# Fill matmuls of the identity with itself on TensorE, ahead of waits, in a one-core encoder kernel

## The chip, the cores and the metric

The kernel runs on one core of one Trainium2 chip. A core has a matrix engine (TensorE, PE in the rows; its weight loads are PEld), VectorE (DVE), ScalarE (ACT), GpSimd (POOL) and SyncE (SP), which run side by side and wait for one another through semaphores, and 16 DMA engines. The metric is the device time of one launch in microseconds (us). For a profiled execution the profile gives the span from the first to the last instruction, and the run its time, which has what lies around the span too.

TensorE's clock is granted at one of two levels, 1.2 or 2.4 GHz. The rows name it as PEclk, 0.50 or 1.00 of full speed for a stretch; a mean lies between.

## The reference

One encoder layer in fp32, applied to two sequences of their own, a prompt of 256 tokens and a sample of 512, model width 1024:

```python
h = rmsnorm(x, norm_mix_g)
q, k, v, z_sg, gate_logits = split(h @ w_in)
attn_branch = block_attention(rope(rmsnorm(q)), rope(rmsnorm(k)), v) @ w_attn_o
sg_branch = spatial_gating(gelu(z_sg), sg_norm_g, sg_w, sg_b) @ w_sg_o
x = x + (sigmoid(g_a) * attn_branch + sigmoid(g_s) * sg_branch) @ w_out
x = x + cross_attention(rmsnorm(x, norm_xa_g), rmsnorm(mem, norm_mem_g), wq_xa, wkv_xa, wo_xa)
x = x + peer_ffn(rmsnorm(x, norm_ffn_g), w_peer_q, peer_k1, peer_k2, expert_down, expert_up)
```

Self-attention has 16 query heads and 4 key heads of 64; cross-attention 4 heads of 256 over 256 memory rows. `peer_ffn` picks, for each token and each of 8 heads, 16 of 16384 experts and sums their rows with gates. A last rmsnorm gives the two outputs.

## The kernel before

Tokens are tiles of 128. The prompt (2 tiles) goes first and the sample (4 tiles) second through the same stages, called the first and the second pass here (`q.first` is true in the first; `NT` is 2 or 4): `mixer_inputs` (L561 to 753), `self_attention`, `mixer_outputs`, `cross_inputs`, `cross_attention`, and then `routing` in the first pass or `routing_and_gates` in the second. `experts` and `final_norm` follow once for all tokens. Each stage writes one instruction stream for each engine; a stream runs in the order in which it is written, and an instruction behind a wait waits too.

Three helpers carry most of TensorE's work.

- `project_tokens` and `project_features` multiply a turned activation by streamed weights. A weight chunk of 512 columns comes in two halves; ScalarE writes a half's high part (`split_hi`, L182, w_hi) and VectorE its low part (`split_lo`, L188, w_lo), and each product is three fp32r matmuls (`three`, L203 to 205). Ahead of each half TensorE waits for the low part (`lo_done`, L214), and from the second chunk on it also waits, tile by tile, until the tile's bank of the chunk before is read out (`o.freed`, L217).
- `Turn` transposes a token-major tile into feature-major blocks in 8 steps of up to 4 tiles, with six banks in turn (L276): ScalarE copies each step out as T_hi (L284), VectorE writes T_lo (L292), and from step 6 on TensorE waits for the T_lo of the step six before. `turn.wait` waits for the last.
- In `self_attention` a step of the loop issues the scores of pair `step`, then the turn (transposes, L947) of pair `step - 2`, then the values (L959) of pair `step - 3`. In the generic `attention` that cross-attention uses the order is the same, with L807, L816 and L827. They differ in what the scores wait for:

```python
                if p >= 2:
                    pe.wait_ge(exped, 2 * p - 2)      # self_attention, scores(p)
                if u >= 3:
                    pe.wait_ge(exped, u - 2)          # attention, scores(u)
```

In the second pass VectorE also does background work: products of gathered expert rows (L135), a number of them written at fixed places of its stream (`bg.dve`), whose rows GpSimd fetches by indirect DMA into a ring of six.

In `mixer_outputs` the attention output projection (evicted at L1161 with a gate), eight spatial-gating matmuls (L1107, evicted at L1179), the turn of their result, the second projection, the turn of the gated sum and the output projection follow one another.

Of the kernel before, what the change touches and what calls it, by code (L numbers as in the profile page):

```python
# [16 lines left out]
P = 128  # L17
# [5 lines left out]
NT = (SAMPLE + PROMPT) // P  # L23
# [181 lines left out]
    return pe.matmul(out, lhs[1], rhs[0], start=False, stop=stop, skip_group_check=True)  # L205


def project_tokens(pe, st, h0, nchunks, T, tiles, lin, o, between=None):

    n = len(tiles)  # L210
    for c in range(nchunks):
        for half in range(2):
            h = h0 + 2 * c + half
            pe.wait_ge(st.lo_done, h + 1)  # L214
            for i, t in enumerate(tiles):
                if half == 0 and c > 0:
                    pe.wait_ge(o.freed, n * (c - 1) + i + 1)  # L217
                for k in range(HK):
                    cols = slice(t * P, (t + 1) * P)
                    kk = half * HK + k  # L220
                    last = three(pe, lin[:, i, :], (T[0][:, kk, cols], T[1][:, kk, cols]),
                                 (st.hi[:, h % 2, k, :], st.lo[:, h % 2, k, :]),
                                 start=(kk == 0), stop=(kk == KB - 1))
                if half == 1:
                    last.then_inc(o.ready, 1)
                elif i == n - 1:
                    last.then_inc(st.used, 1)
                if half == 0 and between is not None:
                    between(c, i)
# [28 lines left out]
class Turn:  # L258
# [6 lines left out]
        (self.turned, self.base), (self.hi, _), (self.lo, _) = (  # L265
            m.carried(x, len(self.steps)) for x in ("turned", "turn_hi", "turn_lo"))

    def pe(self, pe, before=None):

        for n, (k, t0, nt) in enumerate(self.steps):  # L270
            if before is not None:
                before(n, t0 + nt)
            if n >= 6:
                pe.wait_ge(self.lo, self.base + n - 5)
            for t in range(nt):
                last = pe.transpose(self.lin[:, n % 6, t * P:(t + 1) * P],  # L276
                                    self.src[:, t0 + t, k * P:(k + 1) * P], self.ident[:])
            last.then_inc(self.turned, 1)
# [235 lines left out]
def mixer_inputs(nc, block, st, q, bg, x_in, T, Y, qT, kT, v_sb, lin, tr, A, U, GA, GS, stage, ident, gains, choice=None, norm=None, routed=None):  # L514
    NT, H = q.nt, q.h0
    Y = Y[:, q.t0:q.t0 + NT, :]
    Pool.next_stage()

    with ExitStack() as ctx:
# [48 lines left out]
        @block.tensor  # L568
        def _(pe):
            if q.first:  # L570
                pe.wait_ge(turn_in, 32)
            turn.pe(pe, lambda n, end: pe.wait_ge(norm.scaled, norm.base + end))
            turn.wait(pe)
            if not q.first:
                routed(pe)

            def qk_turn(n):
                pe.wait_ge(roped, n + 1)
                if n >= 2:
                    pe.wait_ge(copied, n - 1)  # L580
                for b in range(4):
                    last = pe.transpose(tr[:, n % 2, b * P:(b + 1) * P], rope[:, n % 2, b * P:(b + 1) * P], ident[:])
                last.then_inc(turned, 1)

            def between(c, i):
                if 1 <= c <= 3:
                    qk_turn((c - 1) * NT + i)

            project_tokens(pe, st, H, 11, T, range(NT), lin, o, between)
# [186 lines left out]
def attention(nc, block, tag, bg, T, ident, lin, tr, units, heads, outs, width_of, scores_of, crossed):  # L776
# [8 lines left out]
    with ExitStack() as ctx:  # L785
# [14 lines left out]
        @block.tensor  # L800
        def _(pe):
            def scores(u):
                if u >= 3:
                    pe.wait_ge(exped, u - 2)
                pairs = scores_of(units[u])
                for i, (a, b) in enumerate(pairs):
                    last = pe.matmul(lin[:, u % 3, 0:width_of(units[u])], a, b, start=(i == 0),  # L807
                                     stop=(i == len(pairs) - 1))
                last.then_inc(scored, 1)

            def turn(u):
                pe.wait_ge(normed, u + 1)
                if u >= 3:
                    pe.wait_ge(copied, u - 2)
                for kb in range(width_of(units[u]) // P):
                    last = pe.transpose(lin[:, 3 + u % 3, kb * P:(kb + 1) * P],  # L816
                                        probs[:, u % 3, kb * P:(kb + 1) * P], ident[:])
                last.then_inc(turned, 1)

            def values(u):  # L820
                pe.wait_ge(copied, u + 1)
                h, t = head_of[units[u][:2]], units[u][2]
                for p in (p for p in outs if p["head"] == h):
                    if t == 0 and p["opens"] and p["bank"] >= 2:
                        pe.wait_ge(out_lo, p["bank"] - 1)
                    for kb, v in enumerate(p["values"]):
                        last = pe.matmul(tr[p["rows"], p["bank"] % 2, t * P:(t + 1) * P], v, pT[:, u % 3, kb, :],  # L827
                                         start=(kb == 0), stop=(kb == len(p["values"]) - 1))
                last.then_inc(valued, 1)

            crossed(pe)
            for step in range(N + 3):
                if step < N:
                    scores(step)
                if 2 <= step < N + 2:
                    turn(step - 2)
                if 3 <= step:
                    values(step - 3)
# [69 lines left out]
def self_attention(nc, block, q, bg, T, qT, kT, v_sb, ident, lin, tr, projected):  # L908

    with ExitStack() as ctx:  # L910
# [14 lines left out]
        def _(pe):  # L925
# [40 lines left out]
            for step in range(N + 3):  # L966
                if step < N:
                    scores(step)
                if 2 <= step < N + 2:
                    turn(step - 2)  # L970
                if 3 <= step:
                    values(step - 3)
# [66 lines left out]
        return attended  # L1039


def mixer_outputs(nc, block, st, q, bg, T, Y, G, lin, A, U, GA, GS, ident, cleared, attended, spills_done):
    NT, H = q.nt, q.h0 + 2 * W_AO
    Y = Y[:, q.t0:q.t0 + NT, :]

    with ExitStack() as ctx:
# [50 lines left out]
        @block.tensor  # L1097
        def _(pe):
            attended(pe)
            project_tokens(pe, st, H, 2, T, range(NT), lin, o)  # L1100
            norm.wait(pe)
            pe.wait_ge(small_in, 48)
            pe.wait_ge(o.freed, NO)
            for g in range(G_SG):
                if g >= 6:
                    pe.wait_ge(sg_done, g - 5)
                pe.matmul(lin[:, g % 6, 0:q.n], sgw[:, g, :], Y[:, :, g * P:(g + 1) * P], start=True,  # L1107
                          stop=True).then_inc(sg_ready, 1)
            pe.wait_ge(sg_done, G_SG)
            turn_s.pe(pe)  # L1110
            turn_s.wait(pe)
            project_tokens(pe, st, H + 4, 2, T, range(NT), lin, o2)

            def summed(n, end):
                pe.wait_ge(side_used, NT + end)
                if n < NT:
                    pe.wait_ge(o2.freed, NT + n + 1)
            turn_g.pe(pe, summed)
            turn_g.wait(pe)
            project_tokens(pe, st, H + 8, 2, T, range(NT), lin, o3)  # L1120

# [80 lines left out]
        return norm_m, mixed  # L1202


def cross_inputs(nc, block, st, q, bg, T, Y, G, keysT, vals, lin, A, ident, gains, norm_m, mixed, cleared):
    NT, H = q.nt, q.h0 + 2 * W_XKV
    Y = Y[:, q.t0:q.t0 + NT, :]
    with ExitStack() as ctx:
# [14 lines left out]
        @block.tensor  # L1223
        def _(pe):
            if not q.first:
                pe.wait_ge(cleared, 1)
            norm_m.wait(pe)
            mixed(pe)
            turn_m.pe(pe)
            turn_m.wait(pe)  # L1230
            project_features(pe, st, H, 2, T, PAIRED, lin, o_k)
            pe.wait_ge(o_k.freed, 8)
            project_tokens(pe, st, H + 4, 2, T, range(NM), lin, o_v)
            pe.wait_ge(o_v.freed, 2 * NM)
            norm_x.wait(pe)
            turn_x.pe(pe)
            turn_x.wait(pe)
            project_features(pe, st, H + 8, 2, T, q.features, lin, o_q)

# [68 lines left out]
def routing(nc, block, st, q, bg, x_in, T, Y, G, H, E12, GATE, IDX, lin, tr, A, ident, gains, attended):  # L1308
# [4 lines left out]
    with ExitStack() as ctx:  # L1313
# [21 lines left out]
        def _(pe):  # L1335
# [3 lines left out]
            def normed(n, end):  # L1339
                pe.wait_ge(norm.scaled, norm.base + end)  # L1340
                if n < NT:
                    pe.wait_ge(o_x.freed, NT + n + 1)
            turn.pe(pe, normed)
            turn.wait(pe)
            pe.wait_ge(small_in, 48)

# [99 lines left out]
def routing_and_gates(nc, block, st, q, bg, T, Y, G, H, E12, GATE, IDX, WD, lin, tr, A, ident, gains, attended):  # L1446
# [10 lines left out]
    with ExitStack() as ctx:  # L1457
# [77 lines left out]
        def _(pe):  # L1535
# [3 lines left out]
            def normed(n, end):  # L1539
                pe.wait_ge(norm.scaled, norm.base + end)  # L1540
                if n < NT:
                    pe.wait_ge(o_x.freed, NT + n + 1)
            turn.pe(pe, normed)
            turn.wait(pe)
            pe.wait_ge(small_in, 64)

# [617 lines left out]
def layer(nc, A, outs):  # L2164
# [3 lines left out]
    with ExitStack() as ctx:  # L2168
# [10 lines left out]
        with ExitStack() as c1:  # L2179
# [8 lines left out]
            with nc.Block() as block:  # L2188
                for q in passes:
                    with ExitStack() as c2:  # L2190
# [4 lines left out]
                                                              GS, stage, ident, gains, *carried)  # L2195
                        attended = self_attention(nc, block, q, bg, T, qT, kT, v_sb, ident, lin, tr, projected)
                    norm_m, mixed = mixer_outputs(
                        nc, block, st, q, bg, T, Y, G, lin, A, U, GA, GS, ident, cleared, attended, spills_done)
                    with ExitStack() as c2:
                        k = Pool(nc, c2)  # L2200
                        keysT, vals = k.sb("keysT", [P, KB, MEM]), k.sb("vals", [P, NM, D])
                        crossed = cross_inputs(nc, block, st, q, bg, T, Y, G, keysT, vals, lin, A, ident, gains, norm_m, mixed,
                                               cleared)
                        attended = cross_attention(nc, block, q, bg, T, G, keysT, vals, ident, lin, tr, crossed)
                    if q.first:
# [64 lines left out]
```

## Time and profile before

| what | value |
|---|---|
| time, median of 3 runs | 2790.08 us (2788.72 to 2797.03) |
| time of the profiled execution | 2795.08 us |
| its span | 2793.1 us |
| PE busy | 2431.1 us (87%), x12865 |
| PEld busy | 2095.7 us (75%), x12865 |
| DVE busy | 2256.2 us (81%) |
| ACT busy | 1108.5 us (40%) |
| POOL busy | 1359.3 us (49%) |
| mean granted TensorE clock | 0.947 |
| HBM | 267 GB/s over the span |

The first pass runs from 0 to about 513 us of the span, the second to about 1690 us, and the experts to 2780 us. A busy TensorE in these figures is not TensorE at its full clock: the mean granted clock says that part of the span ran, or idled, at the lower level. In rows of a timeline the columns are start, duration, engine, line, operation, out and in, shape, number of merged instructions, and in brackets the idle time of the engine before them with what ended it.

### The profile page before, as it was taken

What the parts mean: (1) busy time and instruction counts of PE and PEld (TensorE: products, weight loads), DVE (VectorE), ACT (ScalarE), POOL (GpSimd) and SP (SyncE); (2) the same over time, 40 slices, a digit from 0 to 9 for tenths busy, and PEclk for the clock granted to TensorE, in tenths of its full rate; (3) what the DMA queues carried; (4) which work ended last, traced back from release to release, by engine and by line L of the source; (5) the groups of instructions that cost most, each with busy time, mean ns of one, the idle gap of its engine ahead of it and who ended that gap; (6) DMA issues with size and microseconds to landing.
All of it is one profiled execution on the core that took longest, in us unless ns stands there. A gap on an engine that the chain in (4) does not pass through costs nothing. (4 is left out here: it accounts for less than half of the span.)

```text
span 2793.1 us, 37781 instructions
## 1 busy us (share of the span) xinstructions
PE 2431.1 (87%) x12865; PEld 2095.7 (75%) x12865; DVE 2256.2 (81%) x3983; ACT 1108.5 (40%) x1934; POOL 1359.3 (49%) x1054
## 2 busy tenths in 40 slices
PE   6988989799989788888684566999999999999996
PEld 5866778677866566777563556999999999889995
DVE  6445436897688687776899986999999999999998
ACT  4463444333257112333226882333333333333333
POOL 0000000326632444653654435887777777777773
PEclk9999999899999899999897988999999999999998
DMA  4634444226963877875701339999999999999996
GB/s 156 210 118 177 146 156 136 75 87 242 348 247 119 294 267 284 318 265 202 278 31 61 151 134 352 401 400 400 398 400 400 400 400 400 400 400 398 399 400 253
DMA packets 231057, 747.57 MB, mean 268 GB/s; under 512 B 20865, under 2 KB 70065, under 8 KB 214289
## 3 DMA queue, kind: packets, MB, share of 16 engines
q0 software_dynamic: 112288, 408.77, 38.5%
q1 hardware_dynamic: 118640, 337.15, 33.2%
q8 instruction: 73, 1.20, 0.2%
q14 instruction: 56, 0.45, 0.0%
HBM read 708.09 MB, written 37.75 MB: 267 GB/s over the span
## 5 line engine op out<-in xcount | busy, mean ns | idle before, releaser
L1979 POOL DMA_INDIRECT rows<-in_up,now x384 | 591.4, 1540 | 184.2 <-issue 104.2
L147 POOL DMA_INDIRECT row_ring<-in_down,IDX x256 | 346.5, 1354 | 365.8 <-DVE dots L135 306.3
L188 DVE TENSOR_TENSOR w_lo<-w_raw,w_hi 128x2048 fp32r<-128x2048 f32 x116 | 267.2, 2304 | 232.0 <-ACT w_hi L182 231.3
L203 PE MATMUL lin<-w_hi,T_hi 128*128 128x512 f32 x976 | 394.8, 405 | 57.0 <-DVE G L1161 17.1
L2087 DVE SCALAR_TENSOR_TENSOR Y<-rows,dots,Y 128x1024 f32<-128x1024 f32 x320 | 404.3, 1278 | 11.1 <-DMA rows<-in_up,now 7.2
L204 PE MATMUL lin<-w_lo,T_hi 128*128 128x512 f32 x976 | 389.6, 399 | 0.0
L205 PE MATMUL lin<-w_hi,T_lo 128*128 128x512 f32 x976 | 389.0, 399 | 0.0
L182 ACT ACTIVATE w_hi<-w_raw 128x2048 fp32r<-128x2048 f32 x116 | 221.6, 1912 | 371.1 <-PE lin L205 343.1
L203 PE MATMUL tr<-T_hi,d_hi 128*128 128x384 f32 x1024 | 345.8, 338 | 24.7 <-DVE d_lo L2060 24.7
L135 DVE CUSTOM_DVE_ANT_0 row_ring<-row_ring,H 128x1024 f32<-128x1024 f32 x256 | 304.6, 1222 | 64.7 <-DMA row_ring<-in_down,IDX 60.9
L205 PE MATMUL tr<-T_hi,d_lo 128*128 128x384 f32 x1024 | 345.6, 338 | 0.0
L204 PE MATMUL tr<-T_lo,d_hi 128*128 128x384 f32 x1024 | 344.9, 337 | 0.0
L203 PE MATMUL lin<-u_hi,c_hi 128*128 128x512 f32 x768 | 299.1, 389 | 5.4 <-DVE c_lo L2100 5.4
L205 PE MATMUL lin<-u_hi,c_lo 128*128 128x512 f32 x768 | 301.3, 392 | 0.0
L204 PE MATMUL lin<-u_lo,c_hi 128*128 128x512 f32 x768 | 301.1, 392 | 0.0
L203 PEld LDWEIGHTS lin<-w_hi,T_hi 128*128 128x128 f32 x976 | 186.7, 191 | 110.1 <-DVE w_lo L188 31.9
L1979 POOL DMA_INDIRECT rows<-in_down,now x128 | 186.5, 1457 | 69.1 <-issue 32.9
L205 PEld LDWEIGHTS lin<-w_hi,T_lo 128*128 128x128 f32 x976 | 186.6, 191 | 44.2
L204 PEld LDWEIGHTS lin<-w_lo,T_hi 128*128 128x128 f32 x976 | 186.9, 192 | 41.6
L203 PEld LDWEIGHTS tr<-T_hi,d_hi 128*128 128x128 f32 x1024 | 193.9, 189 | 30.1 <-DVE d_lo L2060 25.2
L203 PE MATMUL lin<-T_hi,w_hi 128*128 128x256 f32 (+1 forms) x512 | 174.0, 340 | 34.1 <-DVE w_lo L188 22.8
L204 PEld LDWEIGHTS tr<-T_lo,d_hi 128*128 128x128 f32 x1024 | 193.8, 189 | 4.9
(279 smaller groups left out, 4685.0 us busy)
## 6 DMA issues: line engine op xcount, KB each, us to landing
w_raw<-in_wall SPq DMA_DIRECT2D x116, 1024.0 KB
raw_d<-in_downT SPq DMA_DIRECT2D x128, 512.0 KB
raw_u<-in_up SPq DMA_DIRECT2D x128, 512.0 KB
wd<-dense_gates SPq DMA_DIRECT2D x32, 768.0 KB
dense_gates<-peer SPq DMA_DIRECT2D x6, 2048.0 KB, 6.3
dense_gates<-w_raw SPq DMA_DIRECT2D x6, 2048.0 KB, 6.7
rows<-in_up,now POOLq DMA_INDIRECT x384
row_ring<-in_down,IDX POOLq DMA_INDIRECT x256
```

The lines of the kernel that those rows point to most:

```text
L135: dve.tensor_tensor_reduce(self.ring[:, k, :], self.ring[:, k, :], self.H[:, r % 2, :], 1.0, 0.0, ALU.mult, ALU.add, self.dots[:, r:r + 1] ...
L147: pool.indirect_dma_start(self.ring[:, r % self.K, :], None, self.table, bass.IndirectOffsetOnAxis(ap=self.IDX[:, r:r + 1], axis=0)).then_ ...
L182: act.activation(self.hi[:, h % 2], self.raw[:, h % 2], ACT.Copy).then_inc(self.hi_done, 1)
L188: dve.tensor_tensor(self.lo[:, h % 2], self.raw[:, h % 2], self.hi[:, h % 2].bitcast(F32), ALU.subtract).then_inc(self.lo_done, 1)
L203: pe.matmul(out, lhs[0], rhs[0], start=start, stop=False, skip_group_check=True)
L204: pe.matmul(out, lhs[0], rhs[1], start=False, stop=False, skip_group_check=True)
L205: return pe.matmul(out, lhs[1], rhs[0], start=False, stop=stop, skip_group_check=True)
L1979: pool.indirect_dma_start(rows[:, k, :], None, table, bass.IndirectOffsetOnAxis(ap=now[:, j % 2, k:k + 1], axis=0)).then_inc(rows_in[k], 16)
L2087: dve.scalar_tensor_tensor(out=into, in0=rows[:, k, :], scalar=dots[:, bass.ds(first_row + r, 1)], in1=into, op0=ALU.mult, op1=ALU.add).th ...
```

## The change

A new helper `keep_busy(pe, out, ident, us)` issues `int(us / 0.22)` plain fp32 matmuls of the 128x128 identity with itself into a part of a bank that nobody reads at that time. They signal nothing. A plain fp32 matmul of this size is two MATMUL instructions and two weight loads, as in L1353. The helper is called

- in `mixer_inputs` at the entry, before the turn (2.0 in the first pass, 9 calls; 12.0 in the second, 54), and in the first pass after the turn and before its last wait (3.5, 15 calls);
- in every `Turn` that is given a spare bank, at step 6 after the step's own `before` and ahead of the wait for T_lo (1.5, 6 calls, for 2 tiles; 2.2, 10 calls, for 4);
- in `self_attention` at step 2, between the scores of pair 2 and the turn of pair 0 (3.5, 15 calls; 6.5, 29 calls);
- in `attention` at step 2 in the same place (2.0, 9 calls; 7.0, 31 calls);
- in `mixer_outputs` through the new argument `fill` of `project_tokens`, at the second chunk's first tile, between the wait for `lo_done` and the wait for `o.freed` (3.5, 15 calls; 10.0, 45 calls); after that projection (0.5, 2 calls; 5.0, 22 calls); ahead of the wait for the last spatial-gating eviction (1.0, 4 calls); ahead of the second turn (1.5, 6 calls; 4.5, 20 calls);
- in `cross_inputs` ahead of the first turn (0.5, 2 calls; 8.0, 36 calls), in `routing` (4.0, 18 calls) and `routing_and_gates` (2.0, 9 calls) ahead of the turn.

Nothing else is moved; `tr` is handed to two more functions. The gate matmuls at the end of `routing_and_gates`, the experts and the final norm are as before.

```diff
+def keep_busy(pe, out, ident, us):
+
+    for _ in range(int(us / 0.22)):
+        pe.matmul(out[:, 0:P], ident[:], ident[:], start=True, stop=True, skip_group_check=True)
+
+
+def project_tokens(pe, st, h0, nchunks, T, tiles, lin, o, between=None, fill=None):
...
             pe.wait_ge(st.lo_done, h + 1)
             for i, t in enumerate(tiles):
                 if half == 0 and c > 0:
+                    if c == 1 and i == 0 and fill is not None:
+                        fill()
                     pe.wait_ge(o.freed, n * (c - 1) + i + 1)
...
-    def pe(self, pe, before=None):
+    def pe(self, pe, before=None, spare=None):
 
         for n, (k, t0, nt) in enumerate(self.steps):
             if before is not None:
                 before(n, t0 + nt)
+            if n == 6 and spare is not None:
+                keep_busy(pe, spare, self.ident, 1.5 if nt == 2 else 2.2)
             if n >= 6:
                 pe.wait_ge(self.lo, self.base + n - 5)
...
-            turn.pe(pe, lambda n, end: pe.wait_ge(norm.scaled, norm.base + end))
+            keep_busy(pe, lin[:, 5], ident, 2.0 if q.first else 12.0)
+            turn.pe(pe, lambda n, end: pe.wait_ge(norm.scaled, norm.base + end), tr[:, 0] if q.first else None)
+            if q.first:
+                keep_busy(pe, tr[:, 0], ident, 3.5)
             turn.wait(pe)
...
                 if step < N:
                     scores(step)
+                if step == 2:
+                    keep_busy(pe, tr[:, 1], ident, 2.0 if N == 8 else 7.0)
                 if 2 <= step < N + 2:
                     turn(step - 2)
...
                 if step < N:
                     scores(step)
+                if step == 2:
+                    keep_busy(pe, tr[:, 1], ident, 3.5 if q.first else 6.5)
                 if 2 <= step < N + 2:
                     turn(step - 2)
...
-            project_tokens(pe, st, H, 2, T, range(NT), lin, o)
+            project_tokens(pe, st, H, 2, T, range(NT), lin, o, fill=lambda: keep_busy(pe, lin[:, 5], ident, 3.5 if q.first else 10.0))
+            keep_busy(pe, lin[:, 5], ident, 0.5 if q.first else 5.0)
...
+            keep_busy(pe, tr[:, 0], ident, 1.0)
             pe.wait_ge(sg_done, G_SG)
-            turn_s.pe(pe)
+            turn_s.pe(pe, spare=tr[:, 0])
...
-            turn_g.pe(pe, summed)
+            keep_busy(pe, lin[:, 5], ident, 1.5 if q.first else 4.5)
+            turn_g.pe(pe, summed, tr[:, 0])
...
             norm_m.wait(pe)
+            keep_busy(pe, lin[:, 5], ident, 0.5 if q.first else 8.0)
             mixed(pe)
-            turn_m.pe(pe)
+            turn_m.pe(pe, spare=tr[:, 0])
...
-            turn_x.pe(pe)
+            turn_x.pe(pe, spare=tr[:, 0])
...
-            turn.pe(pe, normed)
+            keep_busy(pe, lin[:, 5], ident, 4.0)
+            turn.pe(pe, normed, tr[:, 0])
...
-            turn.pe(pe, normed)
+            keep_busy(pe, lin[:, 5], ident, 2.0)
+            turn.pe(pe, normed, tr[:, 0])
```

## Rows read from the trace of the kernel before

**Rows 1.** Stretches of TensorE: us, busy (matmuls), granted clock, DMA share, GB/s

```profile
217.90:221.30 3.40, 2.86 (x7) 0.50 0.76 243
795.80:801.40 5.60, 5.52 (x24) 0.50 0.99 394
943.50:948.30 4.80, 4.71 (x11) 0.50 0.97 350
948.50:955.00 6.50, 6.50 (x30) 1.00 1.02 400
```

**Rows 2.** TensorE's timeline: plain fp32 matmuls of the routing scores

```profile
496.97 2.05 PE L1353 MATMUL tr<-subk,peer_qT 128*128 128x128 f32 x16 [0.75 <-ACT peer_qT L1392]
```

**Rows 3.** Self-attention, second pass: timelines of TensorE, then of VectorE

```profile
795.88 2.08 PE L934 MATMUL lin<-kT,G 64*128 64x256 f32 x8 [8.20 <-ACT att_probs L982]
797.89 1.97 PE L947 MATMUL lin<-ident,att_probs 128*128 128x128 f32 x8
...
801.87 1.23 DVE L1025 TENSOR_REDUCE att_nmx<-lin 128x2 f32<-128x1024 f32 x1 [0.48 <-PE lin L934]
```

**Rows 4.** Self-attention, first pass: TensorE, then VectorE

```profile
164.18 1.23 PE L934 MATMUL lin<-kT,G 64*128 64x128 f32 x8 [4.53 <-ACT att_probs L982]
...
167.69 0.69 DVE L1025 TENSOR_REDUCE att_nmx<-lin 128x2 f32<-128x512 f32 x1 [0.79 <-PE lin L934]
```

**Rows 5.** Attention output projection, first pass: VectorE, then TensorE

```profile
215.40 2.29 DVE L188 TENSOR_TENSOR w_lo<-w_raw,w_hi 128x2048 fp32r<-128x2048 f32 x1
...
218.44 0.76 PE L203 MATMUL lin<-w_hi,T_hi 128*128 128x512 f32 x1 [4.63 <-DVE G L1161]
```

**Rows 6.** The same and the gating after it, second pass: VectorE, then TensorE

```profile
940.55 2.29 DVE L188 TENSOR_TENSOR w_lo<-w_raw,w_hi 128x2048 fp32r<-128x2048 f32 x1
942.76 0.69 DVE L1161 TENSOR_TENSOR G<-lin,side 128x512 f32<-128x512 f32 x1
...
966.68 2.29 DVE L188 TENSOR_TENSOR w_lo<-w_raw,w_hi 128x2048 fp32r<-128x2048 f32 x1
...
943.59 0.76 PE L203 MATMUL lin<-w_hi,T_hi 128*128 128x512 f32 x1 [12.45 <-DVE G L1161]
...
974.95 9.16 PE L1107 MATMUL lin<-Y,sgw 128*128 128x512 f32 x16 [6.63 <-DVE G L1161]
984.95 3.71 PE L276 MATMUL lin<-ident,Y 128*128 128x128 f32 x32 [0.84 <-DVE Y L1179]
```

**Rows 7.** Stretches of TensorE after other waits, columns as in rows 1

```profile
272.80:275.80 3.00, 2.95 (x7) 0.50 0.91 353
...
392.70:398.80 6.10, 6.09 (x21) 0.50 0.40 160
...
974.90:978.90 4.00, 3.95 (x5) 0.50 1.00 392
...
1111.30:1115.50 4.20, 4.13 (x19) 0.50 0.33 129
1323.50:1327.00 3.50, 3.41 (x9) 0.55 0.01 2
1562.00:1602.00 40.00, 23.65 (x184) 0.99 0.31 131
```

**Rows 8.** The turn that opens the second pass: TensorE's timeline, then its stretch

```profile
513.32 6.12 PE L276 MATMUL lin<-ident,Y 128*128 128x128 f32 x32 [14.30 <-DVE Y L337]
...
513.30:521.40 8.10, 6.12 (x32) 0.69 0.23 40
```

**Rows 9.** TensorE's timeline at cross-attention, second pass

```profile
1231.28 0.69 PE L816 MATMUL lin<-ident,xatt_probs 128*128 128x128 f32 x2 [8.56 <-DVE xatt_probs L878]
```

**Rows 10.** The start: a DMA's issue, its KB and time to landing, TensorE's first work

```profile
1.99 0.58 POOL L753 DMA_DIRECT2D gains<-in_gains  x1
...
gains<-in_gains POOLq DMA_DIRECT2D x1, 16.0 KB, 7.1
...
10.29 3.31 PE L276 MATMUL lin<-ident,Y 128*128 128x128 f32 x16 [10.29 <-DVE Y L337]
```

More of the change, by code:

```diff
@@ L205, in three @@
     return pe.matmul(out, lhs[1], rhs[0], start=False, stop=stop, skip_group_check=True)
-def project_tokens(pe, st, h0, nchunks, T, tiles, lin, o, between=None):
+def keep_busy(pe, out, ident, us):
+    for _ in range(int(us / 0.22)):
+        pe.matmul(out[:, 0:P], ident[:], ident[:], start=True, stop=True, skip_group_check=True)
+def project_tokens(pe, st, h0, nchunks, T, tiles, lin, o, between=None, fill=None):
     n = len(tiles)
@@ L1039, in self_attention, with mixer_outputs @@
         return attended
-def mixer_outputs(nc, block, st, q, bg, T, Y, G, lin, A, U, GA, GS, ident, cleared, attended, spills_done):
+def mixer_outputs(nc, block, st, q, bg, T, Y, G, lin, tr, A, U, GA, GS, ident, cleared, attended, spills_done):
     NT, H = q.nt, q.h0 + 2 * W_AO
@@ L1202, in mixer_outputs, with cross_inputs @@
         return norm_m, mixed
-def cross_inputs(nc, block, st, q, bg, T, Y, G, keysT, vals, lin, A, ident, gains, norm_m, mixed, cleared):
+def cross_inputs(nc, block, st, q, bg, T, Y, G, keysT, vals, lin, tr, A, ident, gains, norm_m, mixed, cleared):
     NT, H = q.nt, q.h0 + 2 * W_XKV
@@ L2197, in layer @@
                     norm_m, mixed = mixer_outputs(
-                        nc, block, st, q, bg, T, Y, G, lin, A, U, GA, GS, ident, cleared, attended, spills_done)
+                        nc, block, st, q, bg, T, Y, G, lin, tr, A, U, GA, GS, ident, cleared, attended, spills_done)
                     with ExitStack() as c2:
@@ L2201, in layer @@
                         keysT, vals = k.sb("keysT", [P, KB, MEM]), k.sb("vals", [P, NM, D])
-                        crossed = cross_inputs(nc, block, st, q, bg, T, Y, G, keysT, vals, lin, A, ident, gains, norm_m, mixed,
+                        crossed = cross_inputs(nc, block, st, q, bg, T, Y, G, keysT, vals, lin, tr, A, ident, gains, norm_m, mixed,
                                                cleared)
```

## The prediction

> **What bounds the kernel now.** I read the stretches of TensorE first, then its timeline around each place where the change puts something, then VectorE's there. In the two passes the projections run one matmul behind another; ahead of nearly every stage TensorE stands still, mostly for VectorE, and comes back at the low clock: after the wait of 12.45 us it runs 4.8 us at clock 0.50, 11 matmuls, and then at 1.00, 30 matmuls in 6.5 us [rows 1, 6]. That is 0.436 us a matmul against 0.217 (edges counted in), and of a slow stretch I take 0.46 as loss. Shorter and longer slow stretches stand behind other waits [rows 7]. Their loss is what the change can win, and only where TensorE's end is what the next stage waits for. The experts, 1064 us with the clock up, aren't touched.
>
> **Price of a fill.** A call is two plain fp32 matmuls. 16 of these took 2.05 us [rows 2], 32 of the same width 3.71 us [rows 6], with the last one's drain in both: 0.26 and 0.23 us a call, so 0.224 is taken at the high clock, and twice that, 0.44, at the low one. The 427 calls are 96 us of TensorE. A call costs nothing where TensorE would have stood for longer. So each must be read against the wait ahead of which it really stands.
>
> **Fills that stand behind the wait.** In four places they don't fill the wait.
>
> In self-attention the wait is ahead of the scores of pair 2: 8.20 us in the second pass, 4.53 us in the first, and each ends with L934, not with the turn [rows 3, 4]. The fill comes after these scores, where the turn follows without a pause. Its calls are all on the path, and they begin slow, for the wait is as long as before. Second pass: the fill begins at 797.9; slow up to 801.5 as now [rows 1], 8 calls, then 21 at 0.224, 4.7 us: 806.2. The turn (0.9) and the next scores (1.1) put VectorE's reduction at 808.2 instead of 801.87 [rows 3]: +6.3. Queued behind the fill are the turn, the scores of pair 3 and everything of ScalarE and VectorE that follows them. First pass: begins at 165.4 [rows 4]; slow up to 169.8, if the slow part is as long as the second pass's 5.6 us [rows 1], 10 calls, then 5 fast: 170.9, the reduction at 172.1 instead of 167.69 [rows 4], +4.4; 0.7 comes back, since the steps behind it now run fast: +3.7.
>
> In the attention output projection the wait is for the second chunk's low weights and then for `o.freed`, and `fill` sits between the two. The low weights end 0.75 us (217.69 against 218.44) and 0.75 us (942.84 against 943.59) before TensorE starts now [rows 5, 6]; so only this much is covered. First pass: 15 calls from 217.7, slow up to 221.3 [rows 1], 8 calls, 7 fast: 222.9, +4.5, less 1.3 of slow projection (2.9 us by 0.46): +3.2. Second pass: 45 calls from 942.8, slow up to 948.3 [rows 1], 12.5 calls, the rest at 0.224 for 7.3 us: 955.6, +12.0. The projection then runs fast, -2.2: it ends at 968.3 (974.95 less 6.63 [rows 6]) plus 9.8, 978.1. Here VectorE was late by itself: its background rows held the low weights up to 966.68 [rows 6], so only the last eviction counts. But the 22 calls behind the projection, meant for the 6.63 us that are now 0.7, end at 983.0 instead of a start at 974.95. The gating runs fast then, -2.1 (4.0 us slow [rows 7] and VectorE's last eviction behind it), and the turn starts at 990.9 instead of 984.95: +6.0. The four together: 19.2. All fast they would be 10.6, all slow 34 by the same steps; before's own slow stretches are nearest.
>
> **The entry.** The nine calls wait for the identity and the gains; these land at 1.99 + 7.1 = 9.1, and TensorE starts at 10.29 anyway [rows 10]. Slow, they last to 13.0, and the six in the turn come on top, but the clock should be up by then, and what is late in the turn (2.4 us) comes back in the fast first projection. Between 0 and +2.8; I take +0.3.
>
> **Turns.** VectorE paces them: where it comes straight to the turn, fast transposes win only the first step, 0.3 to 0.4. Ten calls in a turn of four tiles make the last two steps late: step 6 ends 5.4 us after the start (7 x 0.44 + 2.24), and ScalarE and VectorE still have two steps to do. For the spatial-gating turn that is +0.9, and the slow matmuls behind it (about 2 us by 0.46) go: 0.
>
> **Fills that do fit.** 54 calls are 12.1 us in 14.30 [rows 8], 31 are 6.9 in 8.56 [rows 9], and the others are likewise 0.4 to 2.5 us short of their wait. What they win, at most the loss and less where the turn behind them leaves TensorE standing again: cross-attention, 6.1 us slow in the first pass [rows 7], loss 2.8, of which its steps show 2.0; the second pass likewise 1.8. First pass: second projection's end to the output projection 1.2 (3.0 us slow [rows 7], VectorE's share off), three turns 0.3 to 0.1 each, 0.6. Second pass: memory keys 0.8 of 1.9 (4.2 us [rows 7]), for 2 us of waiting remain behind the turn; peer queries 0.9 of 1.6 (3.5 us [rows 7]), the cross queries 0.4. At the opening of the second pass the wait behind the turn grows from 2.0 to about 4 us, since the turn is fast and has no spare: 0. Sum 7.7; the upper bound, all losses at the path, is 16; the lower is 2.
>
> A rule of the Trainium skill speaks against even these. In rows 8 the stretch held 32 transposes and no other matmul after 14.3 us of standing, and its mean clock is 0.69, so the clock rose with transposes alone. "TensorE: Matmul & The Clock Gate", Part 4, says that transpose-mode work doesn't count as busy and that the full clock doesn't engage for it. By the rule every turn would cool the engine again and the sum of gains would be the 3.8 of cross-attention; by the rows it is 7.7. I go by the rows.
>
> **The sum.** 2795.08 + 19.2 + 0.3 - 7.7 = 2806.9 for a profiled execution. The profiled one lay 5.0 above the median of 2790.08, so 2801.9.
>
> **Rivals.**
> 1. All gains stay: no stage comes back slow behind a filled wait, 16 instead of 7.7. For it: TensorE's rest in each wait shrinks to 2.5 us or less. Against: several turns leave it standing for another 2 us. It gives 2793.6, and from 19.5 of gains on there would be no loss at all.
> 2. The lateness is absorbed, the other side: TensorE's delay in self-attention and at the gating falls in time that VectorE needs anyway, as its rows at 966.68 do in part [rows 6]. It decides when VectorE's next item isn't the reduction that waits for L934. Against: the brackets name PE as what ended VectorE's wait [rows 3, 4]. It gives 2790.1 + 0.3 - 7.7 = 2782.7.
> 3. The clock doesn't hold over an identity product, so fills run slow and the waits are overrun: four places 34, and 5 at the second pass's opening, 6 at the entry, 15 elsewhere: 2850. Against: products of one-hot tiles kept 0.99 for 40 us with TensorE busy 59% [rows 7].
> 4. Turns cool the engine, the rule above: gains 3.8, 2805.8.
>
> **Chances.** The forecast 0.60 (2796 to 2808, from the phase in which the clock rises), rival 1 0.17, rival 2 0.11, rival 3 0.04, rival 4 0.08. The range leaves out rivals 2 and 3: 2792 to 2811. About 0.3%, 8.4 us, is what a measurement can tell from no change: below 2781.7 only the better part of rival 2, 0.06; up to 2798.5 most of rival 1 (0.13), the rest of rival 2 (0.05) and 0.11 of the forecast, 0.29 in all; above it 0.65.
>
> **What would show it.** L934 of pair 2 followed by 29 identity products and the turn about 8 us later than now; the same between the second chunk's w_lo and its first matmul, 12 us in the second pass; no pause behind the 22; cross-attention's steps at 2.0 us from the first on. If the reduction at L1025 comes as early after the scores of pair 2 as now, or the gating starts where it did, the costs are wrong; if stages behind turns start slow again, the gains are.

## The result and the profile after

The changed kernel takes 2799.67 us (median; 2793.36 to 2807.81) against 2787.19 for the kernel before in the same series: ratio 1.0044, 95% interval 1.0035 to 1.0054. It is slower by 12.5 us, where 2801.9 was forecast from 11.8 us of loss. The profiled execution has a span of 2800.4 us inside a time of 2802.35, a mean granted clock of 0.960 (before: 0.947) and 854 TensorE matmuls more than before, the 427 calls twice. So the clock did come up, and the time with it.

Two rows of the page: the engines' busy us and share of the span, and TensorE's clock in 40 slices:

```profile
PE 2510.0 (90%) x13719; PEld 2183.0 (78%) x13719; DVE 2255.3 (81%) x3983; ACT 1108.1 (40%) x1934; POOL 1365.3 (49%) x1054
...
PEclk9999999999999999999997888999999999999998
```

The line numbers of after are 10 to 20 higher, and each experiment's kernel has its own: L949 is the scores' matmul (before L934), L1042 VectorE's reduction (L1025), L286 a turn's transposes (L276), L1125 the gating (L1107), L1181 the eviction (L1161), L211 the fill. The changed kernel at self-attention in the second pass, TensorE and then VectorE (start, us, operation, in brackets the idle time before it), and TensorE's two stretches (bounds, length, PE, PEld, DVE, ACT and POOL busy with counts, granted clock, DMA share, GB/s):

```profile
793.84 2.08 PE L949 MATMUL lin<-kT,G 64*128 64x256 f32 x8 [8.57 <-ACT att_probs L999]
795.84 8.61 PE L211 MATMUL tr<-ident 128*128 128x128 f32 x58
804.28 1.04 PE L962 MATMUL lin<-ident,att_probs 128*128 128x128 f32 x8
...
806.46 1.23 DVE L1042 TENSOR_REDUCE att_nmx<-lin 128x2 f32<-128x1024 f32 x1 [7.12 <-PE lin L949]
...
793.80:799.40 5.60, 5.57 (x24) 4.74 (x25) 5.46 (x11) 2.77 (x8) 0.95 (x1) 0.50 1.02 415
799.40:804.20 4.80, 4.80 (x44) 4.80 (x43) 0.00 (x0) 0.00 (x0) 0.94 (x1) 0.96 0.57 192
```

The wait ahead of the scores of pair 2 is not filled: 8.57 us, where it was 8.20 [rows 3]. The 58 products stand behind these scores, begin at clock 0.50 as the stretch did before [rows 1], and keep VectorE idle for 7.12 us ahead of its reduction, where it waited 0.48 [rows 3]. First pass:

```profile
162.83 1.23 PE L949 MATMUL lin<-kT,G 64*128 64x128 f32 x8 [4.53 <-ACT att_probs L999]
163.99 5.67 PE L211 MATMUL tr<-ident 128*128 128x128 f32 x30
169.49 0.60 PE L962 MATMUL lin<-ident,att_probs 128*128 128x128 f32 x4
...
170.81 0.69 DVE L1042 TENSOR_REDUCE att_nmx<-lin 128x2 f32<-128x512 f32 x1 [5.26 <-PE lin L949]
```

The wait is the same 4.53 us [rows 4]; VectorE's reduction now waits 5.26 us instead of 0.79. The attention output projection, first pass, then second with the 22 calls and the gating behind it:

```profile
218.66 5.24 PE L211 MATMUL lin<-ident 128*128 128x128 f32 x30 [2.86 <-DVE w_lo L188]
223.66 0.48 PE L203 MATMUL lin<-w_hi,T_hi 128*128 128x512 f32 x1
...
946.27 12.06 PE L211 MATMUL lin<-ident 128*128 128x128 f32 x90 [10.56 <-DVE w_lo L188]
980.57 5.07 PE L211 MATMUL lin<-ident 128*128 128x128 f32 x44
985.48 7.03 PE L1125 MATMUL lin<-Y,sgw 128*128 128x512 f32 x16
...
945.00:952.00 7.00, 5.73 (x35) 5.73 (x36) 7.00 (x12) 0.00 (x0) 5.95 (x4) 0.64 0.92 318
```

TensorE stands still for 10.56 us for the low weights, as before up to the end of w_lo, and only then begins the fill; before, it began the projection 0.75 us after that end [rows 6], now 11.8 us. Where the fill fits, it does what it is for. Cross-attention of the two passes:

```profile
393.24 2.17 PE L211 MATMUL tr<-ident 128*128 128x128 f32 x18
396.19 0.44 PE L829 MATMUL lin<-ident,xatt_probs 128*128 128x128 f32 x2 [0.78 <-DVE xatt_probs L893]
...
1230.94 7.08 PE L211 MATMUL tr<-ident 128*128 128x128 f32 x62
1239.86 0.44 PE L829 MATMUL lin<-ident,xatt_probs 128*128 128x128 f32 x2 [1.83 <-DVE xatt_probs L893]
...
395.00:400.00 5.00, 4.22 (x31) 3.73 (x30) 2.90 (x11) 2.72 (x11) 0.00 (x0) 1.00 0.64 215
```

Of the 8.56 us of waiting 1.83 are left, the two transposes behind take 0.44 instead of 0.69 [rows 9], and the clock of the first pass's steps is 1.00 where it was 0.50 for 6.1 us [rows 7].

### The profile page after: what moved, and what is told of

Read it like the earlier page. It is cut to its first block and busy times, and to the rows that moved or that the text cites. A ratio compares the mean times of both kernels' runs of the same rounds, so it can differ in the third digit from the quotient of the medians.

```text
span 2800.4 us, 39480 instructions
## 1 busy us (share of the span) xinstructions
PE 2510.0 (90%) x13719; PEld 2183.0 (78%) x13719; DVE 2255.3 (81%) x3983; ACT 1108.1 (40%) x1934; POOL 1365.3 (49%) x1054
## 5 line engine op out<-in xcount | busy, mean ns | idle before, releaser
L203 PEld LDWEIGHTS lin<-w_hi,T_hi 128*128 128x128 f32 x976 | 185.4, 190 | 80.4 <-issue 11.8
```

The lines of the kernel that those rows point to most:

```text
L203: pe.matmul(out, lhs[0], rhs[0], start=start, stop=False, skip_group_check=True)
```

## The experiments

The theory is the prediction's: the calls of the four fills behind a wait are all on the path, and the others give back a few us. The rivals are that the lateness is absorbed, that the gains are larger or smaller, and that a turn's transposes cool the engine. Ratios are to the kernel before in the same series; `after` is 1.0044 [1.0035, 1.0054].

**Which part costs.** The changed kernel without self-attention's fills:

```diff
-                if step == 2:
-                    keep_busy(pe, tr[:, 1], ident, 3.5 if q.first else 6.5)
```

> The changed kernel without the two fills of self-attention (15 and 29 calls). My theory: they stand behind the wait of the scores of pair 2 and cost 3.7 and 6.3 us there, so this kernel is 10 us under the changed one, at a ratio to before of 1.001 (changed: 1.0044). Rival, the lateness is absorbed by VectorE: nothing is won, 1.0044. In the trace the turn of pair 0 follows the scores of pair 2 at once.

Measured: 1.0016 [1.0003, 1.0030], 0.0028 or 7.8 us under the changed kernel (by the two intervals some 5 us either way), beside 10 expected. Laid instruction by instruction beside the changed kernel's trace, TensorE gains 3.8 us there in the first pass and 7.2 in the second. In the second pass these scores also start 3.5 us earlier for another reason: the wait ahead of them is 5.10 us instead of 8.57, because VectorE was further on with its background rows in this execution. Single traces differ by such amounts, so one trace alone doesn't price a fill. Without the projection's fills:

```diff
-            project_tokens(pe, st, H, 2, T, range(NT), lin, o, fill=lambda: keep_busy(pe, lin[:, 5], ident, 3.5 if q.first else 10.0))
+            project_tokens(pe, st, H, 2, T, range(NT), lin, o)
```

> The changed kernel without the fill inside the attention output projection (15 and 45 calls); the 22 calls behind the projection stay. My theory: the fill costs 3.2 us in the first pass and 6.0 in the second, so this kernel is 9 us under the changed one, ratio to before 1.001. Rival, VectorE's background rows hide it in the second pass: 3 us under it, 1.0033. In the trace the second chunk starts at the eviction of the first tile, slow, and the 22 calls fit into a wait of 6.6 us.

Measured: 1.0008 [0.9998, 1.0017], 10.0 us under the changed kernel, where 9 was expected and 3 by the rival; by the traces 2.6 and 6.2 at the place. With both edits:

> Both left out, so only fills that fit their waits remain. My theory: the gains alone, 7.7 less 0.3 at the entry: ratio to before 0.9974, or 2780 us where before is 2787. Rival, all gains stay: 16 us, 0.994. Rival, turns cool the engine: 3.5 us, 0.9987.

Measured: 0.9982 [0.9966, 0.9997]. Two findings hang on it. The four fills cost 0.0062, 17.3 us, and the two edits alone come to 17.8: within this noise they add up. And what is left of the change is a gain, 5.0 us by the ratio (0.8 to 9.5 by its interval), near the forecast's 7.7; the largest version, 16, is excluded. The interval doesn't tell 7.7 from 3.8.

The opposite, the kernel before with nothing but these four fills:

```diff
+                if step == 2:
+                    keep_busy(pe, tr[:, 1], ident, 3.5 if q.first else 6.5)
...
+            project_tokens(pe, st, H, 2, T, range(NT), lin, o, fill=lambda: keep_busy(pe, lin[:, 5], ident, 3.5 if q.first else 10.0))
```

> The kernel before with only the four fills that stand behind the wait (15 and 29 calls behind the scores of pair 2, 15 and 45 behind the second chunk's low weights), not the 22 calls behind the projection. The kernel that leaves these four out of the changed one came out 17 us under it (0.9982 against 1.0044). Theory, each call there is on the path: self-attention's two cost 10 us as they did in the changed kernel (3.3 + 6.6), the projection's 2 in the first pass and some 2 in the second, where the 22 calls are missing behind it: +14 us, ratio 1.0050 (1.0035 to 1.0065). Rival, it is the fills together that cost, the early ones putting VectorE's rows where the others collide with them: 4 us or less, 1.0015. Second rival, absorbed: 1.000.

Measured: 1.0058 [1.0042, 1.0074], 16.2 us. The two estimates of the four fills, by taking them out and by putting them in alone, agree, and "absorbed" is out, as is the rival by which only the fills together cost (1.0015). In its trace the low weights end at 958.80 and the fill behind them takes 13.12 us; the changed kernel's took 12.06, so more of it ran slow here.

```profile
958.80 13.12 PE L211 MATMUL lin<-ident 128*128 128x128 f32 x90 [11.74 <-DVE w_lo L188]
995.10 7.10 PE L1119 MATMUL lin<-Y,sgw 128*128 128x512 f32 x16 [0.88 <-DVE G L1173]
```

**The price of a call.** Self-attention's fills in the changed kernel at twice their length:

```diff
-                    keep_busy(pe, tr[:, 1], ident, 3.5 if q.first else 6.5)
+                    keep_busy(pe, tr[:, 1], ident, 7.0 if q.first else 13.0)
```

> The changed kernel with self-attention's fills at 31 and 59 calls instead of 15 and 29: 46 more. Theory, all on the path and by then at the high clock, 0.224 us each: +10.3 us, ratio 1.0081 (1.0070 to 1.0092), and the scores of pair 3 begin 3.6 and 6.7 us later. Rival, from some length on VectorE has work of its own to do and half is absorbed: 1.006. Second rival, low clock, 0.44 each: 1.0117.

Measured: 1.0074 [1.0058, 1.0090], 0.0030 or 8.4 us over the changed kernel. TensorE in its second pass:

```profile
803.94 15.07 PE L211 MATMUL tr<-ident 128*128 128x128 f32 x118
818.84 1.04 PE L962 MATMUL lin<-ident,att_probs 128*128 128x128 f32 x8
```

From the fill's start to the turn 14.90 us against 8.44: 30 calls for 6.46, 0.215 each; in the first pass 16 calls for 3.90 (9.40 against 5.50), 0.24 each. Together 10.4 us, and the time's interval holds it. The low clock's 0.44 a call is out; that half is absorbed, 1.006, the interval would allow, but not these starts.

**The place.** The same fills ahead of the wait instead of behind it:

```diff
+                if step == 2:
+                    keep_busy(pe, tr[:, 1], ident, 3.5 if q.first else 6.5)
                 if step < N:
                     scores(step)
-                if step == 2:
-                    keep_busy(pe, tr[:, 1], ident, 3.5 if q.first else 6.5)
...
+            if c == 1 and half == 0 and fill is not None:
+                fill()
             pe.wait_ge(st.lo_done, h + 1)
...
-                    if c == 1 and i == 0 and fill is not None:
-                        fill()
```

> All fills kept, but self-attention's two stand ahead of the scores of pair 2 and the projection's two ahead of the wait for the second chunk's low weights, so all four lie in their waits (8.2, 4.5, 12.5, 4.6 us). My theory: gains of 7.4 as in the kernel with only the fitting ones, plus the slow starts of these four places, 0.7 to 1.2 each in attention and 1.3 in the first pass's projection, nothing in the second pass's, where VectorE's rows hold: 10.5 us under before, ratio 0.9962. Rival, the place of a fill makes no difference: 1.0044. In the trace the scores of pair 2 start at clock 1.00.

Measured: 0.9975 [0.9963, 0.9987]. The same 427 calls cost 12 us in one order and win 7 in the other; "the place doesn't matter" is out. TensorE of this kernel: first pass's self-attention, the second pass's projection, and the stretches in which self-attention and the projection restart:

```profile
158.27 3.62 PE L211 MATMUL tr<-ident 128*128 128x128 f32 x30
162.86 0.71 PE L949 MATMUL lin<-kT,G 64*128 64x128 f32 x8 [0.98 <-ACT att_probs L999]
...
921.40 10.21 PE L211 MATMUL lin<-ident 128*128 128x128 f32 x90
933.18 0.47 PE L203 MATMUL lin<-w_hi,T_hi 128*128 128x512 f32 x1 [1.57 <-DVE G L1181]
...
782.80:789.00 6.20, 6.20 (x52) 5.13 (x50) 5.78 (x9) 2.79 (x8) 2.82 (x3) 1.00 1.02 425
933.00:938.00 5.00, 4.82 (x21) 3.96 (x22) 5.00 (x10) 0.00 (x0) 4.09 (x4) 1.00 0.95 351
```

The scores take 0.71 instead of 1.23, and both stretches are at 1.00. But 0.9975 against the 0.9982 without these fills is not a difference that the intervals show, and the 3 us more that were expected of these places (0.9962) didn't come. In the second pass's self-attention the next wait took what was won, and behind it the clock fell after all: the values (L974) took 1.91 us where they take 1.09 at the high clock.

```profile
785.82 1.13 PE L949 MATMUL lin<-kT,G 64*128 64x256 f32 x8
...
791.25 1.12 PE L962 MATMUL lin<-ident,att_probs 128*128 128x128 f32 x8 [2.21 <-ACT att_probsT L1008]
792.29 1.91 PE L974 MATMUL tr<-att_probsT,v_sb 128*64 128x128 f32 x16
...
793.00:795.00 2.00, 2.00 (x16) 1.58 (x14) 1.53 (x3) 1.86 (x6) 0.20 (x1) 0.50 0.95 338
```

**Transposes as fills.** As the last kernel, with each call's product replaced by two transposes of the identity:

```diff
-        pe.matmul(out[:, 0:P], ident[:], ident[:], start=True, stop=True, skip_group_check=True)
+        pe.transpose(out[:, 0:P], ident[:], ident[:])
+        pe.transpose(out[:, 0:P], ident[:], ident[:])
```

> The kernel with the fills ahead of their waits (0.9975), with each call two transposes of the identity in place of one plain product of it: as many instructions, of the same width. Theory, transposes hold the clock as plain products do: same time within 2 us, ratio 0.9975 (0.9965 to 0.9985), cross-attention's first step of the second pass in fast steps as with the products. Rival (the Trainium skill, TensorE: Matmul & The Clock Gate, Part 4: transposes don't count as busy): every stage comes back slow as in the kernel before, nothing is gained and what the fills overrun at the low clock is lost, 5 to 15 us: 1.002 to 1.005, and the granted clock in the fills is 0.50.

Measured: 0.9971 [0.9957, 0.9985], the same as with products. A stretch of its trace with transposes alone, and what followed when VectorE was later than usual:

```profile
1211.50:1217.10 5.60, 5.60 (x54) 5.60 (x53) 1.54 (x3) 0.27 (x1) 1.92 (x3) 1.00 0.97 341
...
1221.72 0.44 PE L830 MATMUL lin<-ident,xatt_probs 128*128 128x128 f32 x2 [3.37 <-DVE xatt_probs L894]
...
1221.00:1230.00 9.00, 7.65 (x32) 6.59 (x33) 5.16 (x15) 3.00 (x12) 1.89 (x2) 0.62 0.88 309
```

The clock stays at 1.00 under transposes. It fell only behind the rest that followed them: here the wait outlasted the fill by 3.37 us, in the changed kernel by 1.83, and there the step behind ran at the high clock's 0.44.

**The calls in the turns.** As "ahead of the wait", without the six or ten calls ahead of a turn's seventh step:

```diff
-            if n == 6 and spare is not None:
-                keep_busy(pe, spare, self.ident, 1.5 if nt == 2 else 2.2)
```

> The kernel with the fills ahead of their waits (0.9975), without the six and ten calls ahead of a turn's seventh step. Theory: in a turn of four tiles the ten calls hold the last two steps back by 1 to 2 us (the turn ahead of the feed-forward's first projection started 8.0 us later than before and the projection behind it 10.0 later); six such turns carry them in the two passes: 3 to 6 us less, ratio 0.9960 (0.9950 to 0.9970). Rival: they keep the clock for the projection behind the turn, whose first matmuls would be slow for 2 to 4 us without them: 0.998 to 0.999.

Measured: 0.9943 [0.9925, 0.9961], lower than either theory, and the steps of its trace don't explain 9 us. The same kernel in the next series:

> The same kernel as no_spare_in_turns, in one series with the three others of this call, since its ratio of 0.9943 was lower than its trace explains. Theory, the spares cost what the steps show, 2 to 4 us: ratio 0.9955 (0.9945 to 0.9968). Rival, they cost 8 us, with a part in stages where the traces differ by chance: 0.9943 again or lower.

Measured: 0.9964 [0.9948, 0.9980]. So two series of one kernel lie 0.0021 apart, which is what such ratios can tell here. The same edit on the changed kernel:

> The changed kernel with nothing taken out but the six and ten calls ahead of a turn's seventh step. Theory: the spares cost there what they cost in the kernel with the fills ahead of their waits, 3 to 8 us: ratio 1.0025 (1.0010 to 1.0038). Rival, they pay there, since the clock they keep is needed: 1.0044 or more.

Measured: 1.0042 [1.0028, 1.0056], no difference to 1.0044; the expected 3 to 8 us didn't show. And without the four fills as well:

> As no_spare_again, and without the four fills at the long waits altogether. Theory: ahead of the wait they win what the slow stretches behind those waits cost by the steps, some 0.7 and 1.3 us in the first pass and 0.7 and 1.0 in the second, so this kernel is 3 us slower than no_spare_again: ratio 0.0011 above it (0.0003 to 0.0020). Rival, the place behind VectorE's next work hides it: no difference.

Measured: 0.9978 [0.9961, 0.9995], beside 0.9982 with the spares; above the same kernel with the fills ahead of their waits (0.9964) it lies by 0.0014 where 0.0011 was expected, and the two intervals overlap. The traces say why the spares come out near nothing. The turn ahead of the feed-forward's first projection, second pass, in the changed kernel and then without spares:

```profile
1324.21 4.25 PE L286 MATMUL lin<-ident,G 128*128 128x128 f32 x24 [1.90 <-DVE G L347]
1328.26 2.68 PE L211 MATMUL tr<-ident 128*128 128x128 f32 x20
1330.78 1.04 PE L286 MATMUL lin<-ident,G 128*128 128x128 f32 x8
1333.60 0.50 PE L203 MATMUL lin<-T_hi,w_hi 128*128 128x512 f32 x1 [1.79 <-DVE T_lo L302]
```

```profile
1316.86 5.38 PE L284 MATMUL lin<-ident,G 128*128 128x128 f32 x32 [1.90 <-DVE G L345]
1324.24 0.50 PE L203 MATMUL lin<-T_hi,w_hi 128*128 128x512 f32 x1 [2.01 <-DVE T_lo L300]
...
1325.36 0.63 PE L203 MATMUL lin<-T_hi,w_hi 128*128 128x512 f32 x1
```

From the turn's start to the projection it is 9.39 us with the calls and 7.38 without: they hold the last steps back by 2.0. Without them seven matmuls behind it run at 0.43 instead of 0.23, 1.4 us. In this turn the spare costs 0.6 net; over all turns the runs leave it between nothing and a few us.

**Behind the turns.** The calls belong where TensorE waits for the turn's last evictions. As without spares, with 5 to 11 calls there, for each turn as for this one:

```diff
             turn_s.pe(pe)
+            keep_busy(pe, tr[:, 0], ident, 1.1 if q.first else 2.2)
             turn_s.wait(pe)
```

> As no_spare_again, with 5 to 11 calls in each turn moved to the place behind its last transpose, where TensorE waits 1.5 to 3.3 us for ScalarE and VectorE to finish the last steps. Without spares the projections behind the turns restart slow for 2.1 us at 269, 3.0 at 514, 3.0 at 982, 2.6 at 1040, 3.0 at 1159 and 2.6 at 1310: 16.3 us, by 0.46 a loss of 7.5, of which two thirds are taken to reach the path. Theory: 5 us less than no_spare_again, 0.0018 lower (0.0008 to 0.0028). Rival, VectorE's evictions pace these projections' first tiles: no difference. Rival on the other side, the calls overrun the waits and delay the projection: 0.0010 above it.

Measured: 0.9947 [0.9930, 0.9964], median 2769.70 us against 2774.94 of the kernel without them in the same series: 5.2 us, as expected, though the two intervals overlap. The opening of the second pass, without these calls and then with them (turn, fill, projection, the projection's first 3 us):

```profile
507.49 3.71 PE L284 MATMUL lin<-ident,Y 128*128 128x128 f32 x32 [2.24 <-DVE Y L345]
514.32 0.50 PE L203 MATMUL lin<-w_hi,T_hi 128*128 128x512 f32 x1 [3.12 <-DVE T_lo L300]
...
515.00:518.00 3.00, 3.00 (x11) 2.34 (x10) 2.93 (x18) 0.00 (x0) 0.00 (x0) 0.64 0.00 0
```

```profile
500.64 3.71 PE L284 MATMUL lin<-ident,Y 128*128 128x128 f32 x32 [2.26 <-DVE Y L345]
504.19 2.40 PE L211 MATMUL tr<-ident 128*128 128x128 f32 x20
507.46 0.50 PE L203 MATMUL lin<-w_hi,T_hi 128*128 128x512 f32 x1 [0.88 <-DVE T_lo L300]
...
507.00:510.00 3.00, 2.54 (x11) 2.10 (x12) 2.93 (x15) 0.00 (x0) 0.00 (x0) 1.00 0.00 0
```

Turn to projection takes 6.83 and 6.82 us: the calls cost nothing. The clock behind is 1.00 instead of 0.64. This kernel beats the changed one and the one before, whose median in its series it undercuts by 15.7 us (14.8 by the ratio, 10 to 19 by its interval).

## Why the prediction held, point by point

The steps are read by laying the traces of before and after side by side: the shift of a TensorE instruction is its start in after less its start in before, and a step's cost is the shift behind it less the shift ahead of it.

| step | forecast, us | by the shifts, us |
|---|---|---|
| self-attention's fill, second pass | +6.3 | +6.6 |
| the same, first pass | +3.7 | +3.3 |
| projection's fill, first pass | +3.2 | +1.9 |
| projection's fill and the 22 calls, second pass | +6.0 | +3.9 |
| entry | +0.3 | -0.4 |
| cross-attention, first pass | -2.0 | -3.0 |
| cross-attention, second pass | -1.8 | -0.6 |
| opening of the second pass | 0 | 0 |
| feed-forward's entry, second pass (peer queries) | -0.9 | +0.5 |

**The four fills** were the right step: 19.2 forecast, 15.7 by the shifts, 17.3 and 16.2 by the experiments. The doubled fill confirms the price of a call. The term that was mis-sized is the second pass's projection: the fill was to run for 12.8 us after the end of w_lo and ran for 11.8 (946.27 to 958.09), and VectorE came to the end of w_lo about 1.2 us earlier against the work around it than the forecast's standing start. The first pass's missed 1.3 mostly the same way: w_lo ended 1.0 us later than before (218.66) where TensorE ran 2.0 later. The rest of the second pass's step came as worked out: the 22 calls follow the projection without a pause, and the gating takes 7.03 instead of 9.16 [rows 6], 2.1 less.

**The gains** were mis-sized where TensorE isn't the last. The first pass's cross-attention gave its whole loss back, 3.0, more than the 2.0 forecast. The second gave 0.6 of 1.8, and the entry of the feed-forward lost 0.5 instead of winning 0.9, because the ten calls in its turn cost 2.0, which the forecast put beside VectorE's pace for this turn. The other small gains, forecast at 3.0 together, came to about 0.6. The entry's landing was put too late: the fill began at 7.88, not 9.1, and the turn at 11.62, not 13.0.

```profile
7.88 3.90 PE L211 MATMUL lin<-ident 128*128 128x128 f32 x18 [7.88 <-DMA gains<-in_gains]
11.62 1.47 PE L286 MATMUL lin<-ident,Y 128*128 128x128 f32 x12
```

**The sum** came right partly because errors cancelled. The traces of before and after end 7.3 us apart in span, the medians 12.5. Both profiled executions lay above their medians, 7.9 and 2.7 us, which is the 5.2 between. The forecast subtracted 5.0 for before, from the three times then known, so 11.8 of loss met a measured 12.5 in the medians, while by the shifts it was 7.3. In those 4.5 us two errors cancel: the four fills cost 3.5 less than forecast, and all gains with the entry came to 4.1 instead of 7.4, 3.3 less. So the sum was right partly by luck. The 4.5 themselves lie almost all where no edit touches TensorE's stream: 0.9 between 138 and 155, some 2 between 749 and 785, in a projection where TensorE waits now and then for low weights, and 1.6 over the experts. The first stands, at 0.8 to 0.9, in the traces of all twelve experiments too, and 1.3 to 1.4 of the second in ten of them, so they are rather late spots in the one execution of the kernel before than an effect of the fills. The experts took from 5.1 us less to 2.6 more than there from trace to trace. Why these stretches vary stays open.

**The rivals.** All gains stay: the remaining change wins 5.0, not 16; but with the calls behind the turns, and the four fills ahead of their waits, it is 15.7, so about as much was there to be won, but not by the change as it stands; that kernel also has gains of places that the rival's 16 didn't count. Absorbed: out by the fills alone, 1.0058. A clock that doesn't hold over identity products: out by every fill that ran at 0.22 a call. Turns that cool the engine: out by the trace, in which transposes alone kept 1.00 for 5.6 us; the times alone don't tell its 3.8 from 7.7. The Trainium skill, "TensorE: Matmul & The Clock Gate", Part 4, says of transpose-mode work that it doesn't count as busy; the kernel whose fills are transposes measured 0.9971 beside 0.9975 with products, so the measurement decides against that rule here, for the fp32 transposes of this kernel; the page's own durations there are for bf16.

## What to carry to other kernels

A fill only covers a wait that comes after it in the engine's own order: find which instruction carries the wait, and put the fill ahead of that, not at the start of the stage that the wait seems to belong to. A call ahead of a wait was free here as far as it fitted. A call behind one is on the path: the 46 that were added in self-attention cost 0.22 to 0.24 us each. A whole misplaced fill costs somewhat less than its calls, 15.7 us by the shifts for 104 of them, since the work behind it runs faster and other engines' work covers part. And when the clock is kept up, look for the next wait, which may take all of it: self-attention's second pass ran its restart at 1.00, then waited 2.21 us for ScalarE, and its clock was at 0.50 behind that.

## What was not expected of the hardware

The clock can fall late. In the kernel without spares TensorE rested 3.12 us ahead of the projection at 514.32; the first matmuls there ran at the high pitch, 0.23 us each, and only from 515.81 on did eight run at 0.43 us each:

```profile
515.57 0.41 PE L205 MATMUL lin<-w_hi,T_lo 128*128 128x512 f32 x1
515.81 0.61 PE L203 MATMUL lin<-w_hi,T_hi 128*128 128x512 f32 x1
516.21 0.63 PE L204 MATMUL lin<-w_lo,T_hi 128*128 128x512 f32 x1
```

So the slow stretch need not begin at the wait ahead of it. Nor did the length of the rest alone decide: behind 2.21 us in self-attention the clock fell, and behind 2.24 us in the kernel without spares the turn at 507.49 ran its 32 transposes in 3.71 us, at the high clock. And transposes of the identity hold the clock as well as its products do, at the same 0.22 us a call of two.
